# Values and attention outputs turned by VectorE in 32x32 squares, the squares placed by transfers

## What is computed

```
mod = silu(c) @ ada_w + ada_b;  shift, scale, gate = split(mod, 3)
h = rms_norm(x, norm_pre) * (1 + scale) + shift
q, k, v, z = h @ w_in                      # 8 heads; q, k: 2 maps x 128; v, z: 256 a head
p_m = softmax(mask(q_m k_m^T / sqrt(128)))  # mask: key chunk of 64 <= query chunk
o = (p_0 - lam * p_1) @ v                  # lam from lq1, lk1, lq2, lk2
o = rms_norm(o, subln) * (1 - lambda_init) # over the head's 256
y = (o * silu(z)) @ w_out
out = x + gate * rms_norm(y, norm_post)
```

## Time and profile before

| | |
|---|---|
| time, median of 3 runs (lowest to highest) | 1907.08 us (1906.72 to 1908.92) |
| the profiled execution's own time | 1907.34 us |
| its span | 1905.5 us |
| transfers by DMA | 394048 packets, 473.16 MB |
| issues of `v_dr` stores, `z_sb` loads, `s_dr` stores | 64, 64, 64 |

### The profile page before, as it was taken

How to read it: one execution, slowest core, us unless ns; L and a number is a source line. 1 busy time by engine, 2 the same in 40 slices (tenths; PEclk the granted TensorE clock), 3 DMA queues, 4 the chain that set the end, 5 groups by cost and what they waited for, 6 DMA issues and landing times.

```text
span 1905.5 us, 26384 instructions
## 1 busy us (share of the span) xinstructions
PE 1866.0 (98%) x9072; PEld 1540.9 (81%) x9072; DVE 1379.5 (72%) x2028; ACT 810.1 (43%) x1516; POOL 794.4 (42%) x844
## 2 busy tenths in 40 slices
PE   4999999999999999999999999999999999999998
PEld 1488888888888888888888888888888888888886
DVE  3687888886655546787887877878778776569467
ACT  5633333333444433444443444444444445546452
POOL 2076565655644523344344434434443422116023
PEclk9999999999999999999999999999999999999999
DMA  9898898886674698786877778686777679657777
GB/s 354 253 313 279 274 297 278 284 290 232 214 267 160 237 356 263 225 250 192 253 229 227 235 216 252 198 254 212 232 240 221 213 228 291 207 186 257 258 240 265
DMA packets 394048, 473.16 MB, mean 248 GB/s; under 512 B 22614, under 2 KB 268476, under 8 KB 391228
## 3 DMA queue, kind: packets, MB, share of 16 engines
q1 hardware_dynamic: 393632, 471.43, 76.4%
q10 hardware_dynamic: 284, 0.05, 0.0%
HBM read 323.54 MB, written 147.86 MB: 247 GB/s over the span
## 4 chain that ended last, share of the span: by engine, by line
PE 93%; DVE 1%; DMA 1%; ACT 0%; issue 0%; SPq 0%; POOL 0%; DVEq 0%; POOLq 0%; ACTq 0%
PE ps L1752 30%; PE ps L1754 30%; PE ps L1753 30%; PE ps L1885 2%; PE ps L1861 1%; PE ps L1904 1%; PE ps L1721 0%; DMA ubf<-s_dr 0%; DMA z_dr<-cc 0%; PE ps L1833 0%; DVE ring L1310 0%; ACT h L1040 0%; DVE xt L1632 0%; DVE tB L1330 0%; DVE tB L1327 0%
## 5 line engine op out<-in xcount | busy, mean ns | idle before, releaser
L1752 PE MATMUL ps<-blk,ring 128*128 128x512 f32 x1524 | 603.3, 396 | 2.6 <-DVE blk L1357 1.9
L1754 PE MATMUL ps<-blk,ring 128*128 128x512 f32 x1524 | 594.6, 390 | 0.0
L1753 PE MATMUL ps<-blk,ring 128*128 128x512 f32 x1524 | 594.2, 390 | 0.0
L1752 PEld LDWEIGHTS ps<-blk,ring 128*128 128x128 f32 x1524 | 286.3, 188 | 66.0 <-issue 9.7
L1754 PEld LDWEIGHTS ps<-blk,ring 128*128 128x128 f32 x1524 | 286.0, 188 | 60.8
L1753 PEld LDWEIGHTS ps<-blk,ring 128*128 128x128 f32 x1524 | 286.5, 188 | 55.8
L1310 DVE TENSOR_TENSOR ring<-sums,ring 128x512 fp32r<-128x512 f32 x256 | 234.7, 917 | 95.5 <-ACT ring L1006 93.6
L836 POOL TENSOR_TENSOR sums<-raw 128x512 f32<-128x512 f32 x128 | 191.5, 1496 | 226.9 <-DVE ring L1310 206.0
L1006 ACT ACTIVATE ring<-sums 128x512 fp32r<-128x512 f32 x256 | 160.6, 628 | 179.3 <-PE ps L1754 175.6
L1310 DVE TENSOR_TENSOR ring<-raw,ring 128x512 fp32r<-128x512 f32 x192 | 179.2, 934 | 58.9 <-ACT ring L1006 58.5
L836 POOL TENSOR_TENSOR sums<-sums,raw 128x512 f32<-128x512 f32 x128 | 190.2, 1486 | 20.8 <-DVE ring L1310 14.3
(11 more groups left out here) (159 smaller groups left out, 3181.7 us busy)
## 6 DMA issues: line engine op xcount, KB each, us to landing
raw<-in_diff_w_in_dram SPq DMA_DIRECT2D x64, 1024.0 KB, 7.8
d_dr<-cc SPq DMA_DIRECT2D x124, 256.0 KB, 3.2
cc<-d_dr SPq DMA_DIRECT2D x124, 256.0 KB, 4.1
ubf<-s_dr SPq DMA_DIRECT2D x113, 256.0 KB, 5.0
ada<-in_ada_w_dram SPq DMA_DIRECT2D x88, 256.0 KB, 7.3
tb<-in_diff_w_out_dram SPq DMA_DIRECT2D x32, 512.0 KB, 5.5
t_dr<-tb SPq DMA_DIRECT2D x32, 512.0 KB, 4.9
ada<-in_ada_w_dram SPq DMA_DIRECT2D x32, 512.0 KB
```

What stands on the lines that cost most here:

```text
L1752: MM(dst, a_hi, b_hi, start=start, stop=False, skip_group_check=True)
L1753: MM(dst, a_hi, b_lo, start=False, stop=False, skip_group_check=True)
L1754: return MM(dst, a_lo, b_hi, start=False, stop=stop, skip_group_check=True)
```

## The change

TensorE no longer turns the values or the attention outputs. VectorE's transpose works on 32x32 squares: each square is turned in its place, and the squares themselves stay where they are. The transfers put them in their places. The scale by `subln` becomes a row `sub_row` along the features, multiplied in `out_scale`. The transpose of the output goes from `o_sb` into the same half of bank `OB`, and `gate` becomes one multiplication, with `z_sb` loaded in the squares' order. Since a transfer takes one group of 32 partitions, each of these transfers becomes four, with runs of 32 numbers. The layout of `s_dr` changes, and the semaphore counts with it; the loads from it keep their size.

```diff
+        PAIR_STORED = 2 * 16 * (P // SIDE)
@@ store
                     if part == 2:
-                        dst = v_dr[h * SEQ + half * HALF:h * SEQ + (half + 1) * HALF].rearrange("(t p) s d -> p t s d", p=P)
-                        sp.dma_start(dst[:, :, s, m * P:(m + 1) * P],
-                                     src.rearrange("p (t d) -> p t d", t=HT).bitcast(F32)).then_inc(stored[o], 16)
+                        dst = v_dr[h * SEQ + half * HALF:h * SEQ + (half + 1) * HALF, s]
+                        for d in range(0, P, SIDE):
+                            sp.dma_start(dst[:, m * P + d:m * P + d + SIDE].rearrange("(g i) j -> i g j", i=SIDE),
+                                         src[d:d + SIDE].rearrange("i (g j) -> i g j", j=SIDE).bitcast(F32)).then_inc(
+                                             stored[o], 16)
@@ load_z
-                sp.dma_start(z_sb[:, :, :],
-                             z_dr[h * 2:h * 2 + 2, :, qb * P:(qb + 1) * P].rearrange("m p n -> p m n")).then_inc(z_ld, 16)
+                for c in range(0, P, SIDE):
+                    sp.dma_start(z_sb[c:c + SIDE].rearrange("j m (b i) -> j (m b) i", i=SIDE),
+                                 z_dr[h * 2:h * 2 + 2, :, qb * P + c:qb * P + c + SIDE].rearrange(
+                                     "m (b j) i -> j (m b) i", j=SIDE)).then_inc(z_ld, 16)
@@ store_pair
-                sp.dma_start(s_dr[0:4, h, :, p].rearrange("o p n -> p o n"),
-                             ozf.rearrange("p i m n -> p (i m) n")).then_inc(s_st, 16)
+                for c in range(0, P, SIDE):
+                    sp.dma_start(s_dr[h, 0:4 * P, p, c:c + SIDE].rearrange("(o j) i -> j o i", j=SIDE),
+                                 ozf[c:c + SIDE].rearrange("j t m (b i) -> j (t m b) i", i=SIDE)).then_inc(s_st, 16)
                 sp.wait_ge(osum_ok, 4 * (h * PAIRS + p + 1))
-                sp.dma_start(s_dr[4:8, h, :, p].rearrange("o p n -> p o n"), osum[:, :, :]).then_inc(s_st, 16)
+                for c in range(0, P, SIDE):
+                    sp.dma_start(s_dr[h, 4 * P:8 * P, p, c:c + SIDE].rearrange("(o j) i -> j o i", j=SIDE),
+                                 osum[c:c + SIDE].rearrange("j o (b i) -> j (o b) i", i=SIDE)).then_inc(s_st, 16)
@@ VectorE
+            def v_turn(n):
+
+                i, pi = divmod(n, NP)
+                h, o = head_part(i)[0], AT[pi]
+                if h or o:
+                    dve.wait_ge(post_d, 12 * h + o if o else 12 * (h - 1) + 4)
+                dve.wait_ge(ev_d, 3 * GP + NP * (i - GP) + pi + 1)
+                V.transpose(ps[:, VX], cc[:, buffer_of(i, BLOCK[pi])]).then_inc(vt_ok, 1)
+
             def posts(n):
                 for w in (n - 2, n - 1):
                     if w >= NA and w % NP in BLOCK and w == n - lag(w):
                         post_low(w)
+                if n - 1 >= NA and (n - 1) % NP in BLOCK and head_part((n - 1) // NP)[1] == 2:
+                    v_turn(n - 1)
@@ out_scale
-                V.tensor_scalar(o_sb[:, :], ps[:, OB, 0:VD], ofac[:, 0:1], None, ALU.mult).then_inc(o_ok, 1)
+                else:
+                    dve.wait_ge(cols_ok, 2)
+                STT(o_sb[:, :], ps[:, OB, 0:VD], ofac[:, 0:1], sub_row[:, :], ALU.mult, ALU.mult).then_inc(o_ok, 1)
@@ gate
+                dve.wait_ge(o_ok, a + 1)
+                V.transpose(ps[:, OB, VD:2 * VD], o_sb[:, :]).then_inc(oT_done, 1)
+                dve.wait_ge(z_ld, (a + 1) * 16 * (P // SIDE))
+                if a > 1:
+                    dve.wait_ge(s_st, PAIR_STORED * (a // 2))
                 dve.wait_ge(oT_done, a + 1)
-                dve.wait_ge(z_ld, (a + 1) * 16)
-                if a > 1:
-                    dve.wait_ge(s_st, 32 * (a // 2))
-                for m in range(2):
-                    i = STT(ozf[:, a % 2, m], ps[:, OB, VD + m * P:VD + (m + 1) * P], sub8[:, m:m + 1],
-                            z_sb[:, m], ALU.mult, ALU.mult)
-                i.then_inc(ozf_ok, 1)
+                TTV(ozf[:, a % 2], ps[:, OB, VD:2 * VD].rearrange("p (m n) -> p m n", m=2), z_sb[:, :, :],
+                    ALU.mult).then_inc(ozf_ok, 1)
@@ TensorE
-            def v_turn(i, pi):
...
-            def o_turn(h, qb):
...
```

More of the change, by code:

```diff
@@ L16 @@
 CHUNK = 64
+SIDE = 32
 def build(nc, x, c, ada_w, ada_b, norm_pre, norm_post, w_in, w_out, lq1, lk1, lq2, lk2, subln, out):
@@ L232, in build @@
         ofac = at("ofac", [P, 1], F32, z_at)
+        sub_row = at("sub_row", [P, VD], F32, z_at)
         BLK = 2 * KB * HALF * 4
@@ L267, in build @@
         t_dr = dram("t_dr", [2, HEADS, 4, P, HALF])
-        s_dr = dram("s_dr", [8, HEADS, P, PAIRS, P])
+        s_dr = dram("s_dr", [HEADS, 8 * P, PAIRS, P])
         gp_dr = dram("gp_dr", [KT, P])
@@ L421, in build, with parts_stored @@
                  for n in uses if n[0] >= GP}
+        def parts_stored(n):
+            h, k = divmod(n, PARTS_IN)
+            v = 2 * 16 * (P // SIDE)
+            return h * (v + 32 * (PARTS_IN - 1)) + (v + 32 * (k - 1) if k else 0)
         def stored_block(i, b):
-            return stored[ORDER.index(b)], 32 * (i - GP + 1)
+            return stored[ORDER.index(b)], parts_stored(i - GP + 1)
         read = {}
@@ L551, in load_v @@
                     for e in range(4):
-                        sp.wait_ge(stored[e], (h * 4 + 1) * 32)
+                        sp.wait_ge(stored[e], parts_stored(h * PARTS_IN + 1))
                 if a > 1:
@@ L713, in load_unit @@
                     s, h = {P1: 0, P2: 1, P4: 3, P5: 4, P6: 5, P7: 6, P3: 7}[op], u
-                sp.wait_ge(s_st, 32 * PAIRS * (h + 1))
-                sp.dma_start(ubf[k][:, 1, 1], s_dr[s, h].rearrange("p t n -> p (t n)")).then_inc(unit_in[k], 16)
+                sp.wait_ge(s_st, PAIR_STORED * PAIRS * (h + 1))
+                sp.dma_start(ubf[k][:, 1, 1], s_dr[h, s * P:(s + 1) * P].rearrange("p t n -> p (t n)")).then_inc(unit_in[k], 16)
             for n in range(NA, NA + PARTS_IN * NP):
+                if n == NA + 12:
+                    sp.dma_start(sub_row[:, :], subln[None, :].to_broadcast([P, VD])).then_inc(sub_in, 16)
                 if n == NA + 26:
@@ L1282, in _ @@
             V.memset(yss[:, :, :, :], D * EPS).then_inc(yss_c, 1)
-            dve.wait_ge(c_e, 1)
+            dve.wait_ge(c_ok, 2)
             V.tensor_scalar(cexp[:, :], cexp[:, :], 1.0, None, ALU.add).then_inc(c_ok, 1)
-            dve.wait_ge(c_ok, 2)
+            dve.wait_ge(c_ok, 3)
             V.reciprocal(cexp[:, :], cexp[:, :]).then_inc(c_ok, 1)
-            dve.wait_ge(c_ok, 3)
+            dve.wait_ge(c_ok, 4)
             TTV(cact[:, :], craw[:, :], cexp[:, :], ALU.mult).then_inc(c_ok, 1)
@@ L1557, in _ @@
                 take(n)
+            dve.wait_ge(sub_in, 16)
+            V.tensor_scalar(sub_row[:, :], sub_row[:, :], (1.0 - LAMBDA_INIT) / 2, None, ALU.mult).then_inc(cols_ok, 1)
             n = NA + PARTS_IN * NP
@@ L1727, in ada_rows @@
                 if s == 0:
-                    pe.wait_ge(c_ok, 4)
+                    pe.wait_ge(c_ok, 5)
                 pe.wait_ge(*ada_landed(s))
@@ L1844, in slot @@
             def slot(n, js=range(KB)):
-                if js.start == 0 and n - 2 >= NA and (n - 2) % NP in BLOCK:
-                    f, fp = divmod(n - 2, NP)
-                    h, part = head_part(f)
-                    if part == 2:
-                        v_turn(f, fp)
                 if n < NALL:
                     product(n, js)
-            def v_turn(i, pi):
-                h, _ = head_part(i)
-                b, o = BLOCK[pi], AT[pi]
-                pe.wait_ge(*read_out(i, pi))
-                if h or o:
-                    pe.wait_ge(post_d, 12 * h + o if o else 12 * (h - 1) + 4)
-                for t in range(HT):
-                    last = TR(ps[:, VX, t * P:(t + 1) * P], cc[:, buffer_of(i, b), t * P:(t + 1) * P], ident[:, :])
-                last.then_inc(vt_mm, 1)
             def scores(h, qb, m):
@@ L1898, in weighted @@
                 last.then_inc(pv_done, 1)
-            def o_turn(h, qb):
-                a = h * NB + qb
-                pe.wait_ge(o_ok, a + 1)
-                for m in range(2):
-                    last = TR(ps[:, OB, VD + m * P:VD + (m + 1) * P], o_sb[:, m * P:(m + 1) * P], ident[:, :])
-                last.then_inc(oT_done, 1)
-            def before(a):
-                return divmod(a - 1, NB)
             for n in range(NA, NA + PARTS_IN * NP):
@@ L1921, in _ @@
                         n += 1
-                    if a:
-                        o_turn(*before(a))
                     cut = 1 if qb == HT - 1 else 0
@@ L1972, in _ @@
                     scores(LH, qb, 1)
-                o_turn(*((LH, qb - 1) if qb else (LH - 1, NB - 1)))
                 for i in range(n1):
```

17 lines of the change are left out of this document (7 added, 10 removed).

## The result

| | before | after |
|---|---|---|
| median (lowest to highest) | 1907.30 us (1906.72 to 1908.92), 4 runs | 2032.22 us (2031.6 to 2033.8), 4 runs |
| ratio, 95% interval | | 1.0655 (1.0636 to 1.0673) |
| the profiled execution, its span | 1907.34, 1905.5 us | 2031.6, 2029.7 us |

The change costs 125 us, 6.5%. The prediction was 1950 (1900 to 2080), +43: the right side and inside the range, but only a third of the change.

A forecast was written before the change was run, and what follows sets the result against it. The prediction took TensorE, busy 98% of the span, as the bound: 1907.34 us less 28.5 of turns gives 1878.8, plus 60 (seven stalls), 4 (head 0 and after head 7) and 8 (clock), rounded to 1950 us, range 1900 to 2080.

The forecast's parts named there:

- TensorE, removed: Value turns at 0.45 us and output turns at 0.22 us leave TensorE: 28.5 us gained if nothing makes it wait.
- VectorE: Added transposes, less a shorter gate, put 5.0 us on each head, hidden in VectorE's idle time: counted 0.
- The place: End of the value part: the load of C22's partial sums goes out late, delaying TensorE's weighted sum without reserve.
- SyncE's queue, the price: 27 more issues at 0.50 us against 6.1 us of waits: stalls of 8.5 us in seven heads, +60 us.
- The clock: TensorE's granted clock might drop to its lower level with the stalls: 0 to 30 us, 8 taken.
- Sum: 1878.8 + 60 + 4 + 8 = 1951, rounded to 1950 us.
- Rival 1: Small packets make the DMA engines the bound, above 20.3 ns a packet; 2108 us at 29.8 ns; 18 in 100.
- Rival 2: SyncE's queue absorbs the short issues or has hidden reserve: 1879 us without stall, up to 1902; 15 in 100.

The follow-up runs named there:

- e11: Kernel before with only the outputs turned by VectorE, the partial sums' load ahead of the projections' stores, gate loads of heads 0 to 6 in ScalarE's gap: 1910.9 us.
- e3: Kernel before with value stores, gate loads and pair stores each cut into four by 32 partitions, rows of 512 bytes kept, turns still on TensorE: 1981.6 us.
- e4: Kernel before with value and pair stores in runs of 128 bytes, the old number of issues, gate loads untouched: 1987.9 us.
- e13: e11 with VectorE scaling the previous block's output after combining the probabilities instead of ahead of it, in blocks 0 to 3 of heads 0 to 6: 1918.0 us.

## Why the prediction was right in kind and wrong in size

The step that failed is the price of the stall in SyncE's queue: 60 us in the sum, 98.6 measured. Beside it three smaller terms were off: a second stall had no term (14.1 us measured), the clock was put at 8 us (19 measured), and the gain of the turns at 28.5 (22 measured).

- **TensorE, removed: a quarter too much.** The two places of the earlier trace rows gave 0.45 and 0.22 us a turn. In the six stretches at full clock the same turns took 2.2 us where these prices give 2.9, and in e11 eight output turns 1.2 where they give 1.8. At 2.2 for 2.9 the whole gain is 22 us (an estimate from these rows), not 28.5.
- **VectorE: right to count 0 for the long stalls, sizes right.** The transposes take 722 and 446 ns, for 690 and 476 taken. In the rows of the groups after:

```profile
L1555 DVE STREAM_TRANSPOSE ps<-o_sb 128x256 f32<-128x256 f32 x64 | 28.6, 446 | 0.0
L1522 DVE STREAM_TRANSPOSE ps<-cc 128x512 f32<-128x512 f32 x32 | 23.1, 722 | 0.5
```

  "Hidden" was too simple, though. In e11 some 1.2 us a head is lost in short waits of TensorE, and whether VectorE's added work makes them stays open.
- **The place: right.** The seven stalls are at the load of partial sums ahead of the weighted sum, through the same chain.
- **SyncE's queue, the price: this is the term that failed.** Forecast 8.5 us a stall, measured 14.1 in the mean. Three parts of the working failed. The 27 added issues were priced at 0.50 us; the 39 now there take 0.63 in the mean, and against the earlier trace rows the added ones take 0.66 (24.7 us less the 6.9 us that the twelve held the queue, over 27): 4.3 us more. The price of 0.50 was not wrong in itself: e3, with the issues and without the small packets, has 7.9 us for the working's 7.4. The working said "the engines are hidden behind the queue, barely" and stopped: e4 shows that small packets hold up the issues, and so lengthen the queue itself. And the queue was taken to enter the stretch on time. It had not waited since 1045 us in that head, and came in late: 1.6 us beyond the 1.3 us of TensorE's earlier arrival, and that only because TensorE had been stopped and slowed in the same stretch. 8.7 + 4.3 + 1.6 = 14.6.
- **A second stall, not foreseen.** The gate waits for its own split load, and TensorE for it: 0.7 to 3.1 us a head, 14.1 us in all (112.7 less 98.6). The working has no term for it.
- **The clock: range right, value wrong.** I took 8 us out of 0 to 30, nearer to a row that had no stall in it. By the granted clock of the 8 us behind each stall it was 19: 14 behind the seven long ones (1.4 to 2.6 us each) and 5 behind three of the short ones (1.7 each). TensorE's busy time agrees: 1863.8 us, where 1866.0 less 22 were due. And the loss does not come with the length of the stall, as the upper bound had assumed: 14.6 us of idling gave 4.3 us at the lower level, and the 2.3 us ahead of 1070.69 still some 3, as these rows of TensorE show (products of 128x512 start 0.43 us apart, at the full clock 0.23), while the 2.3 us ahead of 1455.38 gave none:

```profile
1070.69 0.35 PE L1784 MATMUL ps<-v_sb,aT_hi 128*128 128x256 f32 x1 [2.29 <-DVE aT_lo L1578]
...
1072.44 0.63 PE L1785 MATMUL ps<-k_sb,q_sb 128*128 128x512 f32 x1
1072.87 0.63 PE L1786 MATMUL ps<-k_sb,q_sb 128*128 128x512 f32 x1
```

- **Sum, against the profiled execution's 2031.6:** 1907.3 - 22 (turns) + 98.6 (stalls) + 14.1 (second stall) + 19 (clock) = 2017. Some 14 us are left, where 4 were forecast. They are other idle time of TensorE: one stall of 3.9 us in head 0, at 743 us, where the load of partial sums was late too, 4.6 us of waits for the probabilities, and idle stretches of about 1 us.
- **Rival 1, the DMA engines as the bound: wrong as a bound.** The queue's row of the DMA view, from 968.66 to 1098.30:

```profile
q1 hardware_dynamic: 61420, 25.14, 77.6%
```

  That is 100.6 us of the engines, forecast 101.1. Less the 63.0 of the other packets, taken as before, it leaves 14.7 ns for each of 128 bytes (14.9 taken), and the rival needed 20.3. The Trainium skill, page DMA: Bandwidth & Descriptors, section Specifications, has transfers below 512 bytes off line rate, because the engine reads, modifies and writes. On the rate this trace agrees: a quarter of the bytes takes half of the time; the reason no run shows. The page gives no price, and the one that the prediction let it speak for did not come. The mean share was the wrong thing to look at: small packets cost through issues that are held up, at a mean share of 0.78.
- **Rival 2, the issues too short to matter: wrong.** In e3 a transfer of 64 KB takes 0.48 us of the queue, as much as one of 256 KB, and 27 of them are no longer small. This rival rested on the Trainium skill, page DMA: Bandwidth & Descriptors, section Issuing engines are not separate DMA queues, by which the time to start a transfer is usually small beside the transfer. For one transfer that holds here (0.5 us, and some 2 us from issue to landing for an output's 64 KB in the kernel after); it says nothing of a queue in which many stand in front of one load. What the section says of the engines, that all share the same sixteen, no run here tests: e11's second queue took issue time off SyncE, and its bandwidth was not measured by itself.

## What to carry to other kernels

Splitting a transfer costs a nearly fixed 0.5 us of its queue for each piece (here pieces of 32 to 256 KB), and runs of 128 bytes hold the queue longer again; both are paid by whatever stands last in that queue, here a load that nobody had changed. So before splitting transfers, add up the queue's waits over a whole period of the loop, not only ahead of the place that decides, and leave room for issues that lengthen. Issues may be moved to another engine only into time in which it waits anyway: 9 us of them in ScalarE's path cost as much as the stall that they cured, 2 us in its gap cured that of the outputs. Price a stall with the slow clock behind it: here the long ones, 11 to 15 us, cost 1.4 to 2.6 us more each by the clock, and three of seven short ones, 1.8 to 3.1 us, cost 1.7 us more, nearly their own length.

## What the runs showed of the hardware

- VectorE's transpose of 32x32 squares in float32 runs at the pace of an elementwise pass: 722 ns for 128x512 (0.69 us for a pass over as much), 446 ns for 128x256.
- 128-byte packets cost 14.7 ns of an engine each (an estimate, the other packets taken as before). They move a quarter of the bytes of a 512-byte packet at half of its 29.8 ns.
- The issue of one 256 KB transfer takes 0.51 us with 512 pieces, and with 2048 (e4) 0.52 us in one place and 4.34 right behind it. A quarter of it takes 0.48 us with 128 pieces (e3) and 0.54 with 512 (2.15 for four, after), up to 0.97 where it is held up.
- Behind a long idle stretch of TensorE (14.6 us) the clock was at its lower level at once and for 4.3 us. Behind one of 2.3 us, at 1070.69, it was there for some 3 us, beginning 1 us after the restart, and behind another of 2.3 us, at 1455.38, not at all. In e13 a wait of 2.4 us, at 1133.90, was followed by 5 us at 0.66. Behind the waits of up to 0.9 us in e11 it stayed at 1.00.
